# Output projections of a four-layer transformer kernel: f32 row blocks beside split ones, and modulation steps placed elsewhere

## What is computed

```python
# block 1, even layer (rows and context), then odd layer (rows only)
h, gate = rmsnorm(x, g) * (1 + scale) + shift, ...      # shift, scale, gate = silu(c) @ w_ada + b_ada
q, k, v, ..., g = split(h @ w_in)
y = concat(attention_1, attention_2) * silu(g)          # even: window + differential; odd: latent + neighbourhood
x = x + gate * (y @ w_out)                              # the output projection, 1024 x 1024
# block 2, layer l0 and layer l1, each also with a feed-forward part
x = x + g_m * (mixer(h) @ w_out)
x = x + g_f * ((silu(h @ wg) * (h @ wu)) @ wd)
```

## Time and profile before

| | |
|---|---|
| median of 3 runs | 2246.36 us (2245.2 to 2247.95) |
| profiled execution | 2248.18 us, its span 2246.3 us |
| TensorE busy | 2186.7 us, 12072 matmuls |
| VectorE, ScalarE, GpSimd busy | 1266.0, 841.5, 343.4 us |
| DMA | 225.85 MB, 101 GB/s on average |

### The profile page before, as it was taken

One profiled execution on the slowest core, in us unless ns is written; L12 is line 12 of the kernel. 1 busy time (PEld: TensorE's weight loads), 2 busy tenths in 40 slices (PEclk: granted clock), 3 DMA queues, 4 the chain that ended last, 5 costly groups with the idle time before them and its releaser, 6 DMA issues.

```text
span 2246.3 us, 30698 instructions
## 1 busy us (share of the span) xinstructions
PE 2186.7 (97%) x12072; PEld 1725.9 (77%) x12072; DVE 1266.0 (56%) x2566; ACT 841.5 (37%) x1763; POOL 343.4 (15%) x342
## 2 busy tenths in 40 slices
PE   7999999999999999999999999999999999999998
PEld 5977886687547576888778988887778688888886
DVE  3765676753346437577675655562569836433334
ACT  4366424511124106434375322223433833222343
POOL 2300210000000102020200100004533001000144
PEclk9999999999999999999999999999999999999999
DMA  8210330013242552042210455553322004322231
GB/s 323 85 39 20 130 124 20 10 48 108 84 159 86 139 177 55 11 144 90 79 39 17 136 186 187 187 187 113 104 77 92 20 1 148 128 100 94 94 108 71
DMA packets 58268, 225.85 MB, mean 101 GB/s; under 512 B 20478, under 2 KB 21118, under 8 KB 41740
## 3 DMA queue, kind: packets, MB, share of 16 engines
q1 hardware_dynamic: 58124, 223.88, 29.4%
HBM read 221.76 MB, written 2.10 MB: 100 GB/s over the span
## 4 chain that ended last, share of the span: by engine, by line
PE 86%; DVE 6%; ACT 3%; POOL 2%; issue 1%; DMA 1%; SPq 1%; POOLq 0%; DVEq 0%; ACTq 0%
PE PS L86 81%; PE PS L91 5%; POOL WKr L103 1%; ACT WK L98 1%; DMA GB<-in_ev_ada 1%; DVE ACC L115 1%; DVE WK L108 1%; ACT WK L96 1%; SPq L162 1%; ACT WKr L96 1%; DVE SM L135 0%; DVE WK L115 0%; DVE WK L142 0%; DVE RINGr L103 0%; DVE SM L103 0%
## 5 line engine op out<-in xcount | busy, mean ns | idle before, releaser
L86 PE MATMUL PS<-Hr,RINGr 128*128 128x512 f32 (+1 forms) x1304 | 474.5, 368 | 0.0
L86 PE MATMUL PS<-Hr,GBr 128*128 128x512 f32 (+2 forms) x1396 | 462.9, 382 | 0.3 <-DVE GB L115 0.3
L96 ACT ACTIVATE WK<-PS 128x512 f32<-128x512 f32 (+3 forms) x367 | 186.1, 542 | 396.0 <-PE PS L86 224.4
L86 PEld LDWEIGHTS PS<-Hr,GBr 128*128 128x128 f32 (+1 forms) x1396 | 259.8, 188 | 52.8 <-issue 4.1
L86 PEld LDWEIGHTS PS<-Hr,RINGr 128*128 128x128 f32 x1304 | 245.1, 188 | 41.6
L103 DVE TENSOR_TENSOR RINGr<-RING,GBr 128x1024 fp32r<-128x1024 f32 x148 | 184.0, 1281 | 140.8 <-ACT GBr L96 140.4
L86 PE MATMUL PS<-RING,GB 128*128 128x256 f32 x1152 | 251.1, 379 | 0.0
L115 DVE SCALAR_TENSOR_TENSOR ACC<-ADA,SM,ACC 128x512 f32<-128x512 f32 x280 | 215.7, 791 | 48.9 <-DMA ADA<-in_l_mod 35.7
L86 PEld LDWEIGHTS PS<-RING,GB 128*128 128x128 f32 x1152 | 218.2, 190 | 31.2 <-issue 2.1
L86 PE MATMUL PS<-GBr,WKr 128*128 128x512 f32 (+1 forms) x748 | 238.7, 381 | 2.7 <-POOL WKr L103 2.7
L96 ACT ACTIVATE GBr<-RING 128x1024 fp32r<-128x1024 f32 x158 | 158.3, 1047 | 189.4 <-PE PS L86 189.4
(11 more groups left out here) (236 smaller groups left out, 3014.1 us busy)
## 6 DMA issues: line engine op xcount, KB each, us to landing
ADA<-in_l_mod SPq DMA_DIRECT2D x96, 512.0 KB, 4.2
RING<-in_l_gu SPq DMA_DIRECT2D x44, 1024.0 KB, 5.0
RING<-in_l_wd SPq DMA_DIRECT2D x24, 1024.0 KB, 5.0
RING<-in_ev_in SPq DMA_DIRECT2D x13, 1024.0 KB, 5.9
ADA<-in_od_ada SPq DMA_DIRECT2D x24, 512.0 KB, 3.6
RING<-in_od_in SPq DMA_DIRECT2D x11, 1024.0 KB, 5.5
RING<-in_l_in SPq DMA_DIRECT2D x10, 1024.0 KB, 5.0
RING<-in_l_out SPq DMA_DIRECT2D x8, 1024.0 KB, 5.0
```

The source lines that it names most:

```text
L86: self.last = self.eng.matmul(out, lhsT, rhs, start=start, stop=stop, skip_group_check=True)
L96: self.last = self.eng.activation(out, in_, func, bias=bias, scale=scale)
```

## The change

1. The chunks of `w_out` are laid out anew (`_out` for `_chunks`): chunk j holds 512 columns and four of the eight slices of the inner dimension, so products are 512 wide.
2. The first row tile of a projection (the first two in the even layer) stays f32, 512 wide. For the later ones each product is three of halves. ScalarE rounds y (`round_y`) and the weights (`round_out`) at the start of the stage, VectorE subtracts (`low_y`, `low_out`); the low weights go into the ring over the whole ones, after the last f32 tile's half has used them.
3. In the even projection the modulation calls become 0, 4, 2, 0, 1 steps after tiles 0 to 4 (before 4, 3, 3, 3); in the latent projections 5, 4, 4, 4, 4, 4, 4, 0 after gates 0 to 7 (before 4, 4, -, -, 4, 4, 4, -); the neighbourhood projections get 2 more at their end, and the odd output projection's three calls of 2 go. SyncE's ring loads are interleaved anew.

```diff
+M_STEPS = (5, 4, 4, 4, 4, 4, 4, 0)
+EV_STEPS = (0, 4, 2, 0, 1)
...
+        WHOLE_TILES = {"ev_out": 2, "od_out": 1, "l0_out": 1, "l1_out": 1}
...
+            def out_whole(name, t, j, ks_):
+
+                i, b = FIRST[name] + j, where["out", name, t, j // 2]
+                W = ring_view(i, 4)
+                pe.wait_ge(ring_in[i % NRING], ("ring", i))
+                for k in ks_:
+                    pe.matmul(bank(b), Gt(k, t * 128, (t + 1) * 128), W[:, k % 4, :], k == 0, k == 7)
+
+            def out_halves(name, t, j):
+
+                i, b, part = FIRST[name] + j, where["out", name, t, j // 2], int(t > 3)
+                for k in range(j % 2 * 4, j % 2 * 4 + 4):
+                    pe.wait_ge(dve_value, ("low y", name, k, part))
+                    pe.wait_ge(dve_value, ("low out", i, k % 4 // 2))
+                    (yh, yl), (Wh, Wl) = y_terms(name, k, t), out_terms(i, k % 4)
+                    pe.matmul(bank(b), yh, Wh, k == 0, False)
+                    pe.matmul(bank(b), yh, Wl, False, False)
+                    pe.matmul(bank(b), yl, Wh, False, k == 7)
...
                     for jj in range(2):
-                        b = next_bank(("out", name, t, jj), [(dve_value, ("gated", name, t, jj))])
+                        next_bank(("out", name, t, jj), [(dve_value, ("gated", name, t, jj))])
                         for j in (2 * jj, 2 * jj + 1):
...
+                            if t < WHOLE_TILES[name]:
+                                for k in range(j % 2 * 4, j % 2 * 4 + 4):
+                                    y_ready(k, t)
+                                out_whole(name, t, j, range(j % 2 * 4, j % 2 * 4 + 4))
+                            else:
+                                out_halves(name, t, j)
...
+            def then_od(t):
+                if t < 5:
+                    ada(EV_STEPS[t])
+                if t == 4:
+                    norm_mod("od", [(0, range(4))], by_h)
...
                     fm(i, 8, m, "gm", t0 + m, gated("gm", t0 + m), LOC, Ht, h_od)
-                    if t0 + m not in (2, 3, 7):
-                        ada(4)
+                    ada(M_STEPS[t0 + m])
...
+            def round_y(name, part):
+                for k in range(8):
+                    act.activation(y_high(name, k, part), list(y_whole_and_low(name, k, part))[0], ACT.Copy)
+                    act.then_inc(act_value, ("high y", name, k, part))
+
+            def round_out(name):
+                for i in range(FIRST[name], FIRST[name] + 4):
+                    act.wait_ge(ring_in[i % NRING], ("ring", i))
+                    for h in range(2):
+                        act.activation(out_high(i, h), list(out_whole_and_low(i, h))[0], ACT.Copy)
+                        act.then_inc(act_value, ("high out", i, h))
...
             since(act, "att B")
+            round_y("ev_out", 0)
+            round_out("ev_out")
+            round_y("ev_out", 1)
...
+            def low_y(name, part):
+                for k in range(8):
+                    whole, low = y_whole_and_low(name, k, part)
+                    dve.wait_ge(act_value, ("high y", name, k, part))
+                    dve.tensor_tensor(low, whole, y_high(name, k, part), ALU.subtract)
+                    dve.then_inc(dve_value, ("low y", name, k, part))
+
+            def low_out(name, jj):
+
+                dve.wait_ge(pe_product, ("out", name, WHOLE_TILES[name] - 1, jj))
+                for i in (FIRST[name] + 2 * jj, FIRST[name] + 2 * jj + 1):
+                    for h in range(2):
+                        whole, low = out_whole_and_low(i, h)
+                        dve.wait_ge(act_value, ("high out", i, h))
+                        dve.tensor_tensor(low, whole, out_high(i, h), ALU.subtract).then_inc(dve_value, ("low out", i, h))
+
             def out_proj(name, st, tiles, cds, each, nxt=None, half_=None):
+                low_y(name, 0)
                 for n, t in enumerate(tiles):
                     for jj in range(2):
+                        if t == WHOLE_TILES[name] - 1 and (jj or t == 0):
+                            low_out(name, jj)
                         if jj and t == tiles[-1] and nxt is not None:
                             rest(FIRST[nxt])
                         add(name, st, t, jj, where["out", name, t, jj], cds[0] if t < 4 else cds[1], 2 * n + jj)
                         if half_ is not None:
                             half_(t, jj)
+                    if name == "ev_out" and t == 0:
+                        low_out(name, 0)
+                    elif name == "ev_out" and t == 1:
+                        low_y(name, 1)
                     each(t)
...
-            for loads, steps in ((2, 2), (4, 2), (1, 1), (1, 0)):
+            for loads, tiles in ((2, (0, 1, 2)), (1, (3,)), (3, (4, 5)), (1, (6, 7)), (1, ())):
...
+def _out(w):
+    return np.ascontiguousarray(w.reshape(2, 4, 128, 2, 512).transpose(3, 0, 2, 1, 4)).reshape(4, 128, 2048)
```

More of the change, by code:

```diff
@@ new lines, in out_whole_and_low, with out_terms @@
+        def out_whole_and_low(i, h):
+            z = slice(i % NRING * 2048 + h * 1024, i % NRING * 2048 + h * 1024 + 1024)
+            n = 256 if in_gaps(i, h) else 512
+            return (R[:, z].rearrange("p (k n) -> p k n", n=n) for R in (RING, RINGr))
+        def out_terms(i, z):
+            hi, lo = out_high(i, z // 2), RINGr[:, i % NRING * 2048 + z * 512:i % NRING * 2048 + z * 512 + 512]
+            if in_gaps(i, z // 2):
+                return hi[:, z % 2 * 2:z % 2 * 2 + 2, :], lo
+            return hi[:, z % 2, :], lo
@@ new lines, in y_parts, with y_high @@
+        def y_parts(name):
+            return ((256, 512), (512, 768)) if name == "ev_out" else ((128, 512),)
+        def y_high(name, k, part):
+            if name == "ev_out" and part:
+                return Hr[:, k * 768 + 512:k * 768 + 768]
+            if name == "ev_out":
+                return GBr[:, 14336 + k * 256:14592 + k * 256] if k < 7 else WKr[:, 6144:6400]
+            blocks = Hr[:, 0:6144].rearrange("p (b c) -> p b c", c=512)
+            return blocks[:, k // 2 * 3:k // 2 * 3 + 3, 256 + k % 2 * 128:384 + k % 2 * 128]
@@ new lines, in y_whole_and_low, with y_terms @@
+        def y_whole_and_low(name, k, part):
+            a, b = y_parts(name)[part]
+            both_ = (R[:, k * 768 + a:k * 768 + b] for R in (GB, GBr))
+            return both_ if name == "ev_out" else (R.rearrange("p (t c) -> p t c", c=128) for R in both_)
+        def y_terms(name, k, t):
+            lo = GBr[:, k * 768 + t * 128:k * 768 + t * 128 + 128]
+            if name == "ev_out":
+                return y_high(name, k, t // 4)[:, t % 2 * 128 if t < 4 else (t - 4) * 128:][:, 0:128], lo
+            return y_high(name, k, 0)[:, t - 1, :], lo
@@ L1200, in out_early @@
             def out_early(name, j):
-                i, b = FIRST[name] + j, j // 2
                 if j % 2 == 0:
[L1204 to L1210, removed]
+                    take_bank(j // 2, [(dve_value, ("gated", name, 0, j // 2))])
@@ L1212, in out_proj @@
+                    where["out", name, 0, j // 2] = j // 2
+                out_whole(name, 0, j, range(j % 2 * 4, min(j % 2 * 4 + 4, 7)))
             def out_proj(name, tiles, y_ready, between=None, begun=False):
-                for n, t in enumerate(tiles):
-                    if n == 0 and begun:
+                for t in tiles:
+                    if t == 0 and begun:
                         y_ready(7, 0)
[L1216 to L1220, removed]
+                        for jj in range(2):
+                            out_whole(name, 0, 2 * jj + 1, (7,))
+                            pe.then_inc(pe_product, ("out", name, 0, jj))
@@ L3345, in gpsimd @@
             rope("kr", 0)
-            for t in range(2):
-                ada(4)
+            for t in range(4):
+                ada(M_STEPS[t])
             power(("ckv", 0), n + 1, 4)
@@ L3352, in gpsimd @@
             close(of_pool, "proj M")
-            for t in range(4, 7):
-                ada(4)
+            for t in range(4, 8):
+                ada(M_STEPS[t])
             since(pool, "proj M")
@@ L3596, in sync @@
             ada_until(ADA_AFTER["ev", 5])
-            for t in range(4):
-                ada(3 + (t == 0))
+            for t in range(5):
+                ada(EV_STEPS[t])
             for j in range(4):
@@ L3601, in sync @@
             cur.allowed |= {"od", "l0m"}
-            for loads, steps in ((2, 2), (4, 2), (1, 1), (1, 0)):
+            for loads, tiles in ((2, (0, 1, 2)), (1, (3,)), (3, (4, 5)), (1, (6, 7)), (1, ())):
                 for j in range(loads):
                     load()
-                for j in range(steps):
-                    ada(4)
+                for t in tiles:
+                    ada(M_STEPS[t])
             for _ in STEP_TURNS["M"]:
@@ L3624, in sync @@
             sp.dma_start(fin_at("fin1"), brow(A["fin1"], 1024)).then_inc(fin_in["fin1"], "fin1", 16)
-            ada(2)
-            ada(2)
```

(5 more changed lines are left out.)

70 lines of the change are left out of this document (40 added, 30 removed).

## The result

The changed kernel takes **2222.4 us** (median of 4 runs, 2219.36 to 2225.55) against 2246.95 before (now 4 runs): ratio **0.9891, interval 0.9879 to 0.9902**, 24.5 us less. The forecast was 2218, its own range 2213 to 2223, the range over the rivals 2209 to 2230. In a second submission it took 2221.95 us, ratio 0.9882 (0.9866 to 0.9897). The profiled execution took 2219.36 us, span 2217.6, against 2246.3 before: 28.7 us. Of these 2.0 are gained in the first 47 us, where nothing was changed and where before had a granted clock of 0.96 and after 1.00, and 1.2 in the attention of l1, again unchanged, where before had 0.66 from 1752 to 1757 and after 1.00 in the same work.

What follows compares the result with a forecast made beforehand. TensorE, busy 97% of the span, was taken as the bound; 39.3 us saved less waits of 1.6, 1.6, 3.0, 2.3 and 2.4 gives 28.4 us, forecast 2218 us, own range 2213 to 2223, over the rivals 2209 to 2230.

Steps and rivals of the forecast that it cites:

- The gain on TensorE: Four output projections: 13 split blocks each save 3.02 us, 39.3 us off TensorE.
- So one takes 13.90 us: Output projections: one f32 row block takes 13.90 us, as two blocks of 128 instructions take 27.79 us.
- The splitting hides: Output projections: ScalarE's roundings and VectorE's subtractions, about 12 and 13.5 us per projection, hide behind the f32 blocks.
- Odd projection: Odd output projection: VectorE's pieces are ready before TensorE's first split block needs them; no wait, margin 0.7 to 2 us.
- Rival (a): Whole kernel: everything hides, since load waits could overlap the other engine's and the banks could last; 2207 us, chance 0.2.
- (b): First split blocks: each waits for its last pieces, VectorE subtractions stretched by 0.4 us; 13 us in all, 2231, chance 0.24.
- (c): Output projections: one f32 block can't cover the splitting, 17.4 us exposed per projection; slower than before, 2277, chance 0.04.
- (d): Split blocks: new products run at the f32 rate, 20.8 us a block, kernel 90 us more; chance 0.02.
- Even projection: Even output projection: TensorE waits 1.6 us for tile 3's normalisation before transposing; no wait for the split pieces.
- Tails: Ends of the output projections: the next weights' last half is ready late; 1.6 us in all, nothing to 4.
- Latent projections: Latent projections: moved modulation steps make TensorE wait 3.0 us behind gate 1, 2.3 before latent-query products, 2.4 behind gate 3.
- Neighbourhood projections: Neighbourhood projections: four more steps stand ahead of copies TensorE needs only after four tiles; nothing, or 3 us without cover.

Runs made afterwards that it cites:

- the kernel with the early apply: Against the changed kernel: 2, 3, 4, 4, 4, 4, 5, 1 latent steps and 0, 4, 2, 1, 0 even-projection steps, the last apply one tile earlier; 2218.59 us.

## Why the prediction was right, and where not

The forecast lies 4.4 us below the median and was inside its own range by 0.6 us; two of the four executions lie above that range. The mechanism was the right one, and the sizes were off in both directions.

**The gain on TensorE** was over-sized by a little. "A split block is 48 x 0.2267 = 10.88 us" holds exactly. "So one takes 13.90 us" doesn't: I took a group's length for its pitch. Before, three blocks of l1 begin 41.44 us ahead of the transposes (1813.32 to 1854.76), 13.81 each. So 13 x 2.93 = 38.1 us, not 39.3. And "written 512 wide changes nothing" is off by 0.08 us a block.
The Trainium skill's 215.7 ns between matmuls of 512 columns (TensorE: Matmul & The Clock Gate, "Wait — 56ns, not 53.3ns?"), weighed in the prediction, is not what the new products show: 10.88 / 48 is 226.7 ns.

**The splitting hides**, as worked out in "Odd projection": VectorE's pieces of 1024 columns take 4.63 us for four (forecast 4.72). Rival (a), everything hides, fell by the three waits in the latent projections; with the steps spread it would have been the nearest, at 2213 for its 2207. Rivals (b), (c) and (d) fell: no wait at a first split block, starts 0.227 us apart, no stretched subtraction there. The Trainium skill's lock between VectorE and GpSimd (SBUF — State Buffer, "SBUF: two separate sides") wasn't put to a test: GpSimd had 3.46 us of work in 13 around the odd projection's pieces (938 to 951) and 1.24 in 12 around the last one's. But rival (b)'s effect, a wait for the last pieces, is what two kernels with the steps left in place show, from a cause that I hadn't named, modulation calls ahead of the pieces. I had said of the odd projection that losing its calls "pays for VectorE's pieces", which the 5.09 us show; of the even one I hadn't said what would happen without the move.

**Even projection:** 1.6 us forecast for a late normalisation. Measured 1.3, for another reason. This is TensorE's timeline in the kernel after, and VectorE's around it:

```profile
524.23 0.66 PE L91 MATMUL PS<-CN,WK 128*128 128x128 f32 x4 [0.94 <-DVE SM L115]
525.23 0.66 PE L91 MATMUL PS<-CN,WK 128*128 128x128 f32 x4 [0.34 <-DVE SM L115]
```

```profile
519.77 0.75 DVE L108 TENSOR_SCALAR WK<-X,SM 128x1024 f32<-128x1024 f32 x1 [1.93 <-POOL SM L103]
...
523.10 0.69 DVE L137 TENSOR_REDUCE SM<-PS 128x4 f32<-128x512 f32 x1
```

The normalisation of tile 3 was there at 520.5, when TensorE needed it; what came late were the reductions of the last modulation group (523.10), which stood behind tile 4's additions. The size was right, the step wasn't.

**Tails:** 1.6 forecast; 0.6 measured, all in the odd layer (2.39 us at the last transposes against 1.80); l0 and l1 wait for nothing there.

**Latent projections:** 3.0, 2.3 and 2.4 forecast, 3.24, 1.59 and 3.16 measured, 8.0 in place of 7.7; with 1.7 of clock that leaves 0.7 of the 10.4 spread over the stage. The mechanism, that TensorE waits for what stands behind steps held up by their loads, is shown by the kernel in which the same steps stand elsewhere and all three waits are gone. What the sum lacked is the clock behind the waits. The second execution profiled of this kernel had it at two other places: 8.33 us for 16 products that took 7.03, and 7.43 for 10 that took 4.56. That this makes part of the spread of 6 us between its executions is likely and not shown; of the four the two with a mean granted clock of 0.996 took 2219.36 and 2221.25 us, and those with 0.992 and 0.993 took 2225.55 and 2223.55.

**Neighbourhood projections** at "nothing": 1.2 us lost, of which 0.87 is an apply's TensorE work moved there and regained in the odd projection.

Summed: 38.1 - 1.3 - 0.6 - 10.4 (latent) - 0.3 = 25.5 us, against 24.5 by the medians. The profiles' 28.7 contain the 2.0 of the start and the 1.2 of l1's attention, where before had the lower clock; without them they are 25.5 too. The forecast had 28.4, that is 2.9 more: 1.2 for the block read too long, 2.7 for the latent projections (1.7 of it the clock), 0.3 for the neighbourhood ones, less the 1.3 by which the even projection and the tails were charged too dear. That last part is luck: it hid a third of the errors. The last 1.0, between 25.5 and 24.5, I can't place.

## What to carry over

A step with a wait in it (a load that may be late) costs what is queued behind it on its engine. When such steps are moved, look at what stands directly behind each on the way to the bounding engine, and keep short what stands in front of a result it wants next: 2 + 3 steps behind the first two gates in place of 5 + 4, and the four left over behind the last gate, gave 9 us, a third more than the whole change had. A move that looks like a loss by itself (5 us) can be what makes the other part work (it gained 6, and with the steps spread 15: 2228.55 against 2213.4), so undo each part alone before calling it one. For the gain of an edit on a pipelined engine take the distance between starts, not a group's length.

## What was unexpected of the hardware

**Short waits of TensorE cost more than their length.** In the kernel after the granted clock fell to 0.50 (1.2 GHz) for some 3 us behind waits of 3.24 and 1.59 us, with 8 us of work between them that ran at full rate; without the split behind one of 3.30 us (16 products in 8.49 us for 7.03) and again at one of 2.49; in the kernel with the early apply behind one of 6.26 us. The kernel in which no wait in this stage is above 1.3 us shows 1.00 throughout. Which wait is followed by it isn't the same from one execution to the next: in one of the kernel after, the third wait (3.16 us) was followed by 10 products in 4.56 us, in the other (3.09 us) by the same 10 in 7.43. The extra was 1.7 us in the one and 4.6 in the other (1.3 and 2.9 there, and 0.4 at two short products), and neither TensorE's list of waits nor the page's slices show it; the windows do. Here are the 10 products in that other execution, and below it the same four products of l1's attention in the kernel before and in the kernel after, both behind a wait of 0.93 us:

```profile
630.33 7.43 PE L86 MATMUL PS<-RING,WK 128*128 128x512 f32 x10 [3.09 <-DVE GB L120]
...
1752.60 1.87 PE L86 MATMUL PS<-GB 64*128 64x512 f32 x4 [0.93 <-DVE SM L142]
...
1733.92 1.13 PE L86 MATMUL PS<-GB 64*128 64x512 f32 x4 [0.93 <-DVE SM L142]
```

Between 1752 and 1757 before has a granted clock of 0.66 and after, in the same work, 1.00, though the waits there (0.82 and 0.93 us) are the same in both. So a short wait does not decide it alone, and a comparison of two single executions can carry 1 to 3 us of this.
The Trainium skill (TensorE: Matmul & The Clock Gate, "Part 1: The HAM clock gate") says that idleness of the array puts its clock to half. The windows agree so far, with 0.50 behind these waits, though at 1752 no wait was longer than 0.93 us. A forecast that adds waits of 3 us should carry a term for it.
